# Router on the unnormalised residual, tile by tile, with idle products on PE, in a hybrid block with 32 experts

## The reference, cut to what matters

```python
def rms_norm(x, w):
    y = x * lax.rsqrt(jnp.mean(x * x, axis=-1, keepdims=True) + NORM_EPS)
    return y * w
...
h = h + hybrid_mixer(rms_norm(h, attn_norm_w[l]), mem_n, ...)   # ends in: merged @ w_out
h = h + sparse_moe(rms_norm(h, ffn_norm_w[l]), w_router[l], b_router[l], w1, b1, w2, b2)
out = rms_norm(h, final_norm_w)
...
def sparse_moe(xn, w_router, b_router, w1, b1, w2, b2):
    logits = xt @ w_router + b_router                  # (256, 1024) @ (1024, 32)
    top_vals, top_idx = lax.top_k(logits, TOP_K)       # 4 of 32
    gates = jax.nn.softmax(top_vals, axis=-1)
    ...                                                # tokens sorted by expert
    h = x_pad[tok] @ w1[e] + b1[e]                     # (., 1024) @ (1024, 2048)
    y = clamped_swiglu(h) @ w2[e] + b2[e]              # (., 1024) @ (1024, 1024)
```

## Time and profile before

| | |
|---|---|
| runs of the kernel | 1319.02 us median, 1318.52 to 1319.63, 3 runs |
| profiled execution | 1318.95 us, its span 1317.1 us |
| PE busy | 1221.2 us (93%) |
| DVE, ACT busy | 349.0 us (27%), 199.0 us (15%) |
| DMA | 449.72 MB, mean 341 GB/s |
| chain that ended last | PE 63%, DMA 30%, DVE 4%, ACT 1% |

### The profile page before, as it was taken

How to read it: one execution, slowest core, us unless ns; L and a number is a source line. 1 busy time by engine, 2 the same in 40 slices (tenths; PEclk the granted TensorE clock), 3 DMA queues, 4 the chain that set the end, 5 groups by cost and what they waited for, 6 DMA issues and landing times.

```text
span 1317.1 us, 15444 instructions
## 1 busy us (share of the span) xinstructions
PE 1221.2 (93%) x6534; PEld 599.7 (46%) x6534; DVE 349.0 (27%) x574; ACT 199.0 (15%) x381; POOL 0.2 (0%) x4
## 2 busy tenths in 40 slices
PE   7999989999989999999999889898989989898986
PEld 6886778888553333333323233232323323232322
DVE  2146472211123221231212222121222222121222
ACT  1224522200121110111101011110101011110102
POOL 0000000000000000000000000000000000000000
PEclk9999999999979999999999999999999999999998
DMA  8353201595449999999999999999999999999994
GB/s 340 114 165 131 65 3 34 196 389 197 145 153 399 426 428 426 428 428 429 427 427 428 429 429 428 426 429 429 428 428 428 427 429 428 429 428 428 426 427 197
DMA packets 50799, 449.72 MB, mean 341 GB/s; under 512 B 4512, under 2 KB 17184, under 8 KB 25920
## 3 DMA queue, kind: packets, MB, share of 16 engines
q1 hardware_dynamic: 50272, 447.48, 82.2%
q10 hardware_dynamic: 480, 1.57, 0.4%
HBM read 447.99 MB, written 1.05 MB: 341 GB/s over the span
## 4 chain that ended last, share of the span: by engine, by line
PE 63%; DMA 30%; DVE 4%; ACT 1%; issue 1%; SPq 0%; PEldq 0%; DVEq 0%
PE ps L457 61%; DMA ring<-in_w_exp 30%; DVE ring L1380 0%; PE ps L934 0%; DVE upper L1471 0%; PE ps L692 0%; DMA xrows<-in_x 0%; ACT ring L1134 0%; PE ps L473 0%; ACT factors L1261 0%; DVE upper L1585 0%; PE ps L601 0%; DVE ring L1377 0%; ACT ring L1160 0%; PE ps L842 0%
## 5 line engine op out<-in xcount | busy, mean ns | idle before, releaser
L457 PE MATMUL ps<-ring,upper 128*64 128x512 f32 (+4 forms) x2928 | 572.0, 535 | 40.8 <-DMA ring<-in_w_exp 36.3
L457 PEld LDWEIGHTS ps<-ring,upper 128*64 128x64 f32 (+2 forms) x2928 | 181.6, 137 | 392.0 <-issue 325.6
L457 PE MATMUL ps<-upper 128*64 128x512 f32 (+6 forms) x1624 | 282.3, 441 | 17.0 <-DMA upper<-in_w_exp 8.2
L457 PEld LDWEIGHTS ps<-upper 128*64 128x64 f32 (+3 forms) x1624 | 143.3, 162 | 147.9 <-issue 129.2
L457 PE MATMUL ps<-xT,ring 128*128 128x256 f32 x672 | 150.7, 382 | 0.0
L457 PEld LDWEIGHTS ps<-xT,ring 128*128 128x128 f32 x672 | 127.2, 191 | 18.6 <-issue 1.3
L1668 DVE TENSOR_TENSOR xrows<-xrows,ps 128x1024 f32<-128x1024 f32 x32 | 39.1, 1221 | 314.2 <-PE ps L457 314.2
L1647 DVE TENSOR_TENSOR upper<-ps,merged 128x512 f32<-128x512 f32 x32 | 22.1, 692 | 377.2 <-PEq L911 377.2
L1255 ACT ACTIVATE upper<-upper 128x512 f32<-128x512 f32 x32 | 20.2, 631 | 544.0 <-DVE upper L1650 544.0
L1261 ACT ACTIVATE factors<-ps 64x512 f32<-64x512 f32 x64 | 37.9, 592 | 202.7 <-PEq L929 201.9
L457 PE MATMUL ps<-factors,upper 128*128 128x512 f32 x128 | 63.2, 617 | 1.5 <-ACT factors L1261 1.5
(11 more groups left out here) (210 smaller groups left out, 477.8 us busy)
## 6 DMA issues: line engine op xcount, KB each, us to landing
ring<-in_w_exp SPq DMA_DIRECT2D x142, 2048.0 KB, 32.5
upper<-in_w_exp SPq DMA_DIRECT2D x48, 2048.0 KB, 33.6
ring<-in_w_gate SPq DMA_DIRECT2D x9, 1024.0 KB, 5.1
ring<-in_w_in SPq DMA_DIRECT2D x8, 896.0 KB, 10.5
ring<-in_w_in SPq DMA_DIRECT2D x8, 640.0 KB, 3.9
ring<-in_w_branch SPq DMA_DIRECT2D x5, 1024.0 KB, 5.1
ring<-in_w_mem_kv SPq DMA_DIRECT2D x4, 1024.0 KB, 4.9
ring<-in_w_out SPq DMA_DIRECT2D x4, 1024.0 KB, 14.4
```

What stands on the lines that cost most here:

```text
L457: return pe.matmul(o, l, r, start=start, stop=stop, skip_group_check=True)
```

## The change

The router no longer reads the normalised `hn` but the residual itself. PE transposes `xrows` and DVE copies the result (`hT`); the norm's weights are multiplied into `wrt` beforehand (8 instructions of DVE, from a new column block of the parameters), and the reciprocal root is applied to the logits together with the bias. The residual is added in halves, each with a count of its own. `hn` is still made, for the gather.

The work of the router is done tile by tile. Tile 0 is turned after k = 1 of tile 1's out projection, its router products stand after k = 3, and its rank product after k = 6. The last count of `slots_used` before the experts comes with the first transpose of tile 1. The first gather is in two halves, one a tile. w_router is loaded in one transfer of rows of 32 numbers.

`keep_awake` puts products on PE whose results nobody reads: 7 of 128 columns at the outset once the identity is there, 2 of 256 columns behind the out projection, 3 of 256 before the second half of the gather. At the outset, each tile has its own root and reciprocal.

```diff
-            for b in range(2):
-                sp.dma_start(wrt[:, 4 * b:4 * b + 4, :], w_router[0, b * 512:(b + 1) * 512, :].rearrange("(p c) e -> p c e", c=4)).then_inc(late_loaded, 16)
+            sp.dma_start(wrt, w_router[0].rearrange("(c p) e -> p c e", p=P)).then_inc(late_loaded, 16)
...
+            def keep_awake(n, bank, moving):
+                for _ in range(n):
+                    mm(ps[:, bank, 0:moving.shape[-1]], ident, moving)
+
             pe.wait_ge(ident_loaded, 16)
+            keep_awake(7, 7, ident)
             for t in range(TT):
...
 
                 for c in range(KC):
                     if c % 4 == 0:
-                        pe.wait_ge(hn_sb, 2 * t + c // 4 + 1)
-                        if t == 1 and c == 0:
-                            pe.wait_ge(merged_sb, len(UNITS))
-                    last = pe.transpose(ps[:, 4 + 2 * t + c // 4, (c % 4) * P:(c % 4 + 1) * P], hn[:, t, c * P:(c + 1) * P], ident)
+                        pe.wait_ge(resid, 2 * t + c // 4 + 1)
+                    last = pe.transpose(ps[:, 4 + 2 * t + c // 4, (c % 4) * P:(c % 4 + 1) * P], xrows[:, t, c * P:(c + 1) * P], ident)
                     if c % 4 == 3:
-                        last.then_inc(hnT_ps, 1)
-
+                        last.then_inc(hT_ps, 1)
+                    elif t == 1 and c == 0:
+                        last.then_inc(slots_used, 1)
+
+            def router(t):
+
+                if t == 0:
+                    pe.wait_ge(wr_sb, KC)
+                for c in range(KC):
+                    if c % 4 == 0:
+                        pe.wait_ge(hT_sb, 2 * t + c // 4 + 1)
+                    last = mm(ps[:, 0, t * NE:(t + 1) * NE], hT[:, c, t * P:(t + 1) * P], wrt[:, c, :], t == 0 and c == 0, c == KC - 1)
+                last.then_inc(logit_ps, 1)
+
+            def gather_half(t):
+
+                pe.wait_ge(sel_sb if t else sel0_sb, 1)
+                pe.wait_ge(hn_sb, 2 * t + 2)
+                for c in range(KC):
+                    last = mm(ps[:, 4 + c // 4, (c % 4) * P:(c % 4 + 1) * P], hn[:, t, c * P:(c + 1) * P],
+                              sel[:, t, :, :], t == 0 and c % 4 == 0, t == 1)
+                if t:
+                    last.then_inc(xg_ps, 1)
+
+            before = const("before")
 
             for t in range(TT):
                 for k in range(KC):
@@ -856,32 +881,26 @@
                             last.then_inc(slots_used, 1)
                     if t == 1 and k % 2 and k < KC - 1:
                         last.then_inc(slots_used, 1)
-                    if t == 1 and k == 5:
+                    if t == 1 and k == 1:
                         turn_input(0)
+                    if t == 1 and k == 3:
+                        router(0)
+                    if t == 1 and k == 6:
+                        pe.wait_ge(chosen_sb, 1)
+                        mm(ps[:, 1, 0:NE], before, chosen[:, 0, :]).then_inc(rank_ps, 1)
                 last.then_inc(out_ps, 1)
 
-            for t in range(TT):
-                if t == 1:
-                    turn_input(1)
-                for c in range(KC):
-                    if c % 4 == 0:
-                        pe.wait_ge(hnT_sb, 2 * t + c // 4 + 1)
-                    if t == 0 and c == 0:
-                        pe.wait_ge(late_loaded, 16 * 6)
-                        pe.wait_ge(resid, 1)
-                    last = mm(ps[:, 0, t * NE:(t + 1) * NE], hnT[:, c, t * P:(t + 1) * P], wrt[:, c, :], t == 0 and c == 0, c == KC - 1)
-                    if t == 0 and c == 0:
-                        last.then_inc(slots_used, 1)
-            last.then_inc(logit_ps, 1)
-
-            pe.wait_ge(chosen_sb, 1)
-            before = const("before")
-            mm(ps[:, 1, 0:NE], before, chosen[:, 0, :])
-            mm(ps[:, 1, NE:2 * NE], ones, chosen[:, 0, :], False)
-            mm(ps[:, 1, NE:2 * NE], before, chosen[:, 1, :], False).then_inc(rank_ps, 1)
+            keep_awake(2, 4, const("iota"))
+            turn_input(1)
+            router(1)
+            gather_half(0)
+            pe.wait_ge(chosen_sb, 2)
+            mm(ps[:, 3, 0:NE], ones, chosen[:, 0, :])
+            mm(ps[:, 3, 0:NE], before, chosen[:, 1, :], False).then_inc(rank_ps, 1)
             mm(ps[:, 2, 0:NE], ones, chosen[:, 0, :])
             mm(ps[:, 2, 0:NE], ones, chosen[:, 1, :], False).then_inc(rank_ps, 1)
-
+            keep_awake(3, 7, const("iota"))
+            gather_half(1)
...
+            act.wait_ge(zeroed, 2)
             for t in range(TT):
                 act.wait_ge(x_loaded[t], 16)
                 act.activation(dump[:, t, :], xrows[:, t, :], ACT.Square, accum_out=ss[:, t:t + 1]).then_inc(act_step, 1)
-            act.wait_ge(act_step, 2)
-            act.wait_ge(zeroed, 2)
-            act.activation(ss[:, 4:6], ss[:, 0:2], ACT.Sqrt, scale=1.0 / D, bias=epsc[:, 0:1]).then_inc(root, 1)
+                act.wait_ge(act_step, t + 1)
+                act.activation(ss[:, 4 + t:5 + t], ss[:, t:t + 1], ACT.Sqrt, scale=1.0 / D, bias=epsc[:, 0:1]).then_inc(root, 1)
...
-                act.wait_ge(resid, t + 1)
+                act.wait_ge(resid, 2 * t + 2)
                 act.activation(sq_dump, xrows[:, t, :], ACT.Square, accum_out=ss[:, t:t + 1]).then_inc(ffn_ss, 1)
                 act.wait_ge(ffn_ss, t + 1)
                 act.activation(ss[:, 4 + t:5 + t], ss[:, t:t + 1], ACT.Sqrt, scale=1.0 / D, bias=epsc[:, 0:1]).then_inc(ffn_root, 1)
@@ -1235,11 +1255,7 @@
                     for quarter in range(4):
                         hf = quarter // 2
                         act.dma_start(b1rows[NE * quarter:NE * quarter + NE, :], b_exp1[0, :, hf * D:(hf + 1) * D]).then_inc(b1_full, 16)
-                for b in range(2):
-                    act.wait_ge(hnT_ps, 2 * t + b + 1)
-                    act.activation(hnT[:, 4 * b:4 * b + 4, t * P:(t + 1) * P], ps[:, 4 + 2 * t + b, :].rearrange("p (c t) -> p c t", c=4),
-                                   ACT.Copy).then_inc(hnT_sb, 1)
-            act.wait_ge(top_sb, 1)
+            act.wait_ge(top_sb, TT)
...
-            dve.wait_ge(root, 1)
-            link(dve.reciprocal(ss[:, 4:6], ss[:, 4:6]))
             for t in range(TT):
+                dve.wait_ge(root, t + 1)
+                link(dve.reciprocal(ss[:, 4 + t:5 + t], ss[:, 4 + t:5 + t]))
                 TS(xscaled[:, t, :], xrows[:, t, :], ss[:, 4 + t:5 + t], None, ALU.mult).then_inc(scaled, 1)
...
+            dve.wait_ge(late_loaded, 16 * 5)
+            for c in range(KC):
+                TS(wrt[:, c, :], wrt[:, c, :], col("ffn", c), None, ALU.mult).then_inc(wr_sb, 1)
+
+            def places(q):
+                a = CONST["iota"][0]
+                return cst[:, bass.ds(q * SLOTS + a, SLOTS)].unsqueeze(1).unsqueeze(1).to_broadcast([P, TT, 2, SLOTS])
+
             for t in range(TT):
                 dve.wait_ge(out_ps, t + 1)
-                TTn(xrows[:, t, :].rearrange("p (b n) -> p b n", b=2), xrows[:, t, :].rearrange("p (b n) -> p b n", b=2),
-                    ps[:, 2 * t:2 * t + 2, :], ALU.add).then_inc(resid, 1)
+                for b in range(2):
+                    half = slice(b * 512, (b + 1) * 512)
+                    TTn(xrows[:, t, half], xrows[:, t, half], ps[:, 2 * t + b, :], ALU.add).then_inc(resid, 1)
+                for b in range(2):
+                    dve.wait_ge(hT_ps, 2 * t + b + 1)
+                    dve.tensor_copy(hT[:, 4 * b:4 * b + 4, t * P:(t + 1) * P],
+                                    ps[:, 4 + 2 * t + b, :].rearrange("p (c t) -> p c t", c=4)).then_inc(hT_sb, 1)
                 dve.wait_ge(ffn_root, t + 1)
-                if t == 0:
-                    dve.wait_ge(late_loaded, 16 * 6)
                 link(dve.reciprocal(ss[:, 4 + t:5 + t], ss[:, 4 + t:5 + t]))
-                for b in range(2):
+
+                def normed_half(b):
                     half = slice(b * 512, (b + 1) * 512)
                     STT(hn[:, t, half].rearrange("p (c q) -> p q c", c=4), xrows[:, t, half].rearrange("p (q c) -> p q c", c=4),
                         ss[:, 4 + t:5 + t], ffnw[:, half].rearrange("p (q c) -> p q c", c=4), ALU.mult, ALU.mult).then_inc(hn_sb, 1)
 
-            dve.wait_ge(logit_ps, 1)
-            link(TTn(logit[:], ps[:, 0, 0:TT * NE].rearrange("p (t e) -> p t e", t=TT), brt[:].unsqueeze(1).to_broadcast([P, TT, NE]), ALU.add))
-            for t in range(TT):
-                step(dve.max(top8[:, t, :], logit[:, t, :]))
-            settle()
-            TS(rtmp[:, :, 0], top8[:, :, 0], -1.0, None, ALU.mult).then_inc(top_sb, 1)
-            dve.wait_ge(top_sb, 1)
-            link(dve.memset(top8[:, :, 4:8], 3e38))
-            for t in range(TT):
-                step(dve.match_replace(rest[:, t, :], top8[:, t, :], logit[:, t, :], -3e38))
-            settle()
-            TTn(chosen[:], rest[:], logit[:], ALU.not_equal).then_inc(chosen_sb, 1)
-            dve.wait_ge(chosen_sb, 1)
+                normed_half(0)
+                dve.wait_ge(logit_ps, t + 1)
```

(21 more changed lines are left out.)

16 lines of the change are left out of this document (5 added, 11 removed).

## The result

| | before | after |
|---|---|---|
| runs, first timing | 1319.33 us median (1318.52 to 1319.65, 4 runs) | 1310.01 us median (1309.0 to 1312.36, 4 runs) |
| ratio | | 0.993, 95% interval 0.9918 to 0.9942 |
| profiled execution, its span | 1318.95, 1317.1 us | 1312.36, 1310.5 us |
| mean granted clock of it | 0.988 | 0.994 |
| start of the projections | 11.76 | 12.71 |

The forecast was 1310.3 in 1307.8 to 1315.

The account below looks back on a forecast made before the run. The expert weight stream bounds the kernel, its end set by the first expert product behind the router chain. 1318.95 - 8.2 (router) - 0.6 (outset) = 1310.2, with 0.07 to the median 1310.3 us; range 1307.8 to 1315.

Parts of the forecast that it names:

- The stream follows: Expert weight stream: its end moves with the first expert product, so the whole 8.2 us gain counts.
- the dead stretch: Before expert 0, ring full and DMA still: about 5 us of 15 would be left.
- The chain behind the out projection: From the out projection's end, 368.55, through tile 1's router and gather to the first expert product, 378.7: 10.3 us won.
- The longer out projection: Tile 0's router and rank records inside tile 1's out projection lengthen it by 2.1 us, with no wait of PE.
- The clock held: PE's clock stays up behind the out projection: 1309 to 1312 us, chance 0.64.
- the 8.2 us: Router's gain at the first expert product, 386.9 to 378.7: 10.3 won behind the out projection, 2.1 lost in it.
- The rival's 4.2: Rival where the clock falls behind the out projection: first expert product 382.9 for 378.7, 1314.3 us; chance 0.22.
- The outset: Kernel's start: idle products cost 0.8 us but raise the clock earlier; net gain 0.6, bounds -0.8 and +1.5.
- The size: Whole kernel: gains of 8.2 us in the router and 0.6 at the outset, to 1310.3 us.

Follow-up runs that it names:

- The pad: Changed kernel with 20 more idle products of 256 columns before the gather's second half: 1320.3 us, ratio 1.0002 to the kernel before.
- the third timing: The changed kernel, unaltered, timed a third time against the kernel before: 1312.68 us, ratio 0.9938.
- the second timing: The changed kernel, unaltered, timed again on the chip of three follow-up kernels, against the kernel before: 1313.8 us, ratio 0.9949.
- the normalised rows: Changed kernel with the router reading the normalised rows again, w_router unscaled and in two transfers: 1323.56 us, ratio 1.0026 to the kernel before.

## Why the prediction was right, and where not

**The stream follows: right.** The pad moved the first product by 8.5 us and the span by 7.8. SyncE issued 3.86 or 3.87 us behind the first product in every profile, and the rest took 928 to 932 us. Of the dead stretch about 4 us are left, where I had said 5.

**The chain behind the out projection: right to 0.6 us.** Forecast 10.15 from its end to the first product (368.55 to 378.7), measured 10.7 (368.8 to 379.5). DVE's steps came as worked out (residual 370.09, copies 371.54, choice 374.32 for 374.05). PE's did not: I had eight of the router's records done by 371.4 and the rest by 372.0, but all sixteen ran in one piece from 371.00 (to 372.9 by their rate), so that from there PE, not DVE, ended last: the ranks began at 374.67 for 374.05, and the gather's second half took 1.95 for 1.7.

**The longer out projection: right.** 2.1 forecast; it ends at 368.8, 2.4 later than before, of which 0.4 is the outset's. PE waited nowhere in it.

**The clock held, in the three profiled executions.** Forecast with 0.64. In the three profiles of the changed kernel it was 1.00 from 360 to 390; of its other twelve executions no trace tells. But 5.0 of the 8.2 us can be had by the clock alone, which my sum had inside the durations without naming it: with the clock lost, as in the kernel without idle products, the first product was 4.6 us later. The rival's 4.2 (382.9 for 378.7) was about its size. One reading in it was off: by the earlier trace rows the clock rose 5.8 us behind the gather's start (385.4 for 379.58) and not 5.4.

**The outset: wrong, in sign.** The step was: idle products cost 0.8 and give back 1.4, net +0.6. They cost 2.4 between 10.32 and 12.71, because I compared their end with the transposes' start of the kernel before, 8.32, and not with what the split root makes possible, 6.88. And they brought the clock's rise no earlier: without them it rose as early (10.2 to 12.2, against 10.5 to 12.9). The edit's two parts are +1.4 (root) and -2.4 (products), a loss of 0.95 at the start of the projections, of which the clock gives back some: 0.4 late at 352 in this profile, 0.15 in the second, 2.2 in the third, where the identity landed at 7.03. What came with the earlier rise is PE's earlier start (6.9 to 7.2 in place of 8.3), and transposes were enough for it. In the kernel with one idle product, none of them at the outset, second timing, PE had done nothing but transposes when the clock rose at 10.24:

```profile
7.19 3.42 PE L476 MATMUL ps<-cst,upper 128*128 128x128 f32 x16 [7.19 <-DVE upper L1352]
10.62 5.63 PE L456 MATMUL ps<-xT,ring 128*128 128x256 f32 x25
```

The last two transposes came 0.13 us apart, those before 0.21. The Trainium skill (TensorE: Matmul & The Clock Gate, PE-mode transpose) says that a transpose does not count for the clock as a product does. For these float32 transposes the two rows speak against it.

**The size.** With the router 7.7 us earlier (7.4 at the first product, plus the outset's 0.4), the outset -0.4 and 0.8 lost near 400, the profiled execution gained 6.6. The forecast had 8.2 for the router, +0.6 for the outset and nothing near 400; the parts as measured make 6.6. That the medians of the first timing gave 9.3, close to the forecast's 8.7, is in part luck: the later timings gave 5.8 and 7.6.

**What makes executions differ.** I had expected the third timing's longer executions to show 0.50 behind the out projection. Its profile (1314.03 us; windows as in the earlier trace rows) does not:

```profile
100.00:150.00 50.00, 47.64 (x239) 34.31 (x238) 29.98 (x67) 24.46 (x68) 0.00 (x0) 0.93 0.34 109
150.00:200.00 50.00, 43.08 (x987) 36.02 (x984) 32.56 (x48) 18.21 (x42) 0.00 (x0) 0.93 0.06 22
370.00:380.00 10.00, 9.81 (x72) 8.61 (x71) 7.45 (x22) 3.26 (x6) 0.00 (x0) 1.00 0.73 245
390.00:410.00 20.00, 18.53 (x65) 5.83 (x62) 6.02 (x9) 2.88 (x4) 0.00 (x0) 0.83 0.94 388
```

Against the second timing's profile (1309.65), 1.1 us are lost by the start of the projections, 0.95 more by the first product (the clock low twice for 6.8 us at 112 and 173, once there), and 2.3 behind it (low at 399, there not at all): 4.4, the whole difference. In other executions it may be the router; that stays open, since only one execution a kernel is traced.

## What to carry to other kernels

Where a stream of weights bounds the kernel, look for the stretch in which its ring is full and nothing moves: what ends that stretch sets the end of the kernel, here to within 3.7 us over 14 profiles, and its length says how much there is to win: 14.7 us before, about 4 after. Price an idle product by what PE could do in its place after the whole change, not before it: those at the outset stood in front of work that had come early, those before the gather outlasted the wait that they filled, and one short product of 0.43 us with none of the others was faster than the changed kernel on both chips that had the two (1309.8 against 1313.8, 1309.3 against 1312.7). And when a chain with waits is shortened, count how much of the gain is the clock: here 5.0 of 7.4 us could be had with nine idle products and nothing else.

## What the runs showed of the hardware

The granted clock fell without a long pause of PE: in the kernel without idle products from 370.6 on, after transposes, 32-column records and pauses of 0.8 and 0.2 us, and with half the gather moved from 374.2 on, in a wait of 1.4 us. Nearly the same sequence kept it in the profile of the kernel without idle products in the router, so one profile does not tell whether a wait is safe.

How long it stays low differs as much: 13.7 us in the kernel before, 10.2 without idle products, 6.8 with half the gather moved, and 17.1 with tile 0 behind the out projection, the longest stretch seen. In these four it rose while PE was in the gather's products; with the normalised rows, low for 6.8 us, in the 32-column records of the ranks (386.5).

At the outset 16 float32 transposes alone were followed by the rise. Before its first record of the clock a trace gives 1.00, and there only durations tell the level: 421 ns a transpose at the lower one, 273 at the upper.

The transfer of the identity landed 4.0, 4.5 and 4.9 us after its issue in three profiles of one and the same program. The projections began at 12.71, 12.46 and 13.58, so its landing alone does not set them: in the second the clock rose at 10.5, in the first at 11.7.
